# The byte distance between split weights and the activations they meet, changed from 32, 64, 96 and 128 to 48, 56, 72 and 80

## The reference

```python
def swiglu(h, w_gu, w_down):
    u = h @ w_gu                       # 1024 -> 2 x 2816
    g, v = u[..., :D_FF], u[..., D_FF:]
    return (jax.nn.silu(g) * v) @ w_down   # 2816 -> 1024

h = h + mixer(rmsnorm(h, g0))
h = h + swiglu(rmsnorm(h, g1), w_gu, w_down)   # six of these in all
```

## Time and profile before

| | us |
|---|---|
| median of 3 runs | 1706.4 |
| lowest, highest | 1705.34, 1708.17 |
| the profiled execution: its own time | 1707.63 |
| its span, first to last instruction | 1705.7 |
| outside the span | 1.9 |
| PE busy in the span | 1677.9 (98%) |
| DVE, ACT, POOL busy | 1265.5, 832.6, 375.4 |
| granted TensorE clock, mean | 0.999 of full |

### The profile page before, as it was taken

How to read it: one execution, slowest core, us unless ns; L and a number is a source line. 1 busy time by engine, 2 the same in 40 slices (tenths; PEclk the granted TensorE clock), 3 DMA queues, 4 the chain that set the end, 5 groups by cost and what they waited for, 6 DMA issues and landing times.

```text
span 1705.7 us, 31820 instructions
## 1 busy us (share of the span) xinstructions
PE 1677.9 (98%) x12958; PEld 1576.4 (92%) x12958; DVE 1265.5 (74%) x1657; ACT 832.6 (49%) x1104; POOL 375.4 (22%) x425
## 2 busy tenths in 40 slices
PE   7999999999999999999999999999999999999999
PEld 7789998898789999899989999998999999899998
DVE  7898889785868988788857866666666665676663
ACT  5865444343665444454444255444444445554442
POOL 0223012535505132610032130002100137330000
PEclk9999999999999999999999999999999999999999
DMA  8245567675206788555646445564455544335560
GB/s 321 107 141 211 210 219 262 232 281 190 77 2 205 244 267 300 183 191 194 228 166 235 137 162 177 193 220 176 152 193 204 215 150 168 125 126 198 202 230 33
DMA packets 50711, 321.02 MB, mean 188 GB/s; under 512 B 7696, under 2 KB 8912, under 8 KB 20144
## 3 DMA queue, kind: packets, MB, share of 16 engines
q1 hardware_dynamic: 36432, 280.61, 46.1%
q0 software_dynamic: 12736, 36.87, 6.7%
q10 hardware_dynamic: 1440, 2.10, 0.3%
HBM read 307.39 MB, written 10.09 MB: 186 GB/s over the span
## 4 chain that ended last, share of the span: by engine, by line
PE 87%; DVE 8%; ACT 2%; issue 2%; DMA 1%; POOL 0%; ACTq 0%; DVEq 0%; POOLq 0%
PE bank L2268 18%; PE bank L2262 17%; PE bank L2263 16%; PE bank L2264 16%; PE bank L2269 9%; DVE w_lo L1436 2%; PE bank L2549 1%; PE bank L2916 1%; PE bank L2868 1%; ACT w_hi L1006 1%; PE bank L2734 1%; PE bank L2623 1%; PE bank L2454 1%; PE bank L2559 1%; DVE rstd L1446 1%
## 5 line engine op out<-in xcount | busy, mean ns | idle before, releaser
L1436 DVE TENSOR_TENSOR w_lo<-raw,w_hi 128x1024 fp32r<-128x1024 f32 (+2 forms) x486 | 644.8, 1330 | 259.1 <-ACT w_hi L1006 257.9
L1006 ACT ACTIVATE w_hi<-raw 128x1024 fp32r<-128x1024 f32 (+2 forms) x486 | 538.2, 1117 | 546.7 <-PE bank L2264 323.0
L2262 PE MATMUL bank<-hg_hi,w_hi 128*128 128x256 f32 x2648 | 748.1, 283 | 12.3 <-DVE hg_lo L1441 10.4
L2263 PE MATMUL bank<-hg_lo,w_hi 128*128 128x256 f32 x2648 | 743.6, 281 | 0.0
L2264 PE MATMUL bank<-hg_hi,w_lo 128*128 128x256 f32 x2648 | 742.7, 280 | 0.0
L2262 PEld LDWEIGHTS bank<-hg_hi,w_hi 128*128 128x128 f32 x2648 | 500.6, 189 | 17.6 <-DVE w_lo L1436 11.5
L2264 PEld LDWEIGHTS bank<-hg_hi,w_lo 128*128 128x128 f32 x2648 | 501.1, 189 | 0.0
L2263 PEld LDWEIGHTS bank<-hg_lo,w_hi 128*128 128x128 f32 x2648 | 500.7, 189 | 0.2
L2268 PE MATMUL bank<-hid,w_hi 128*128 128x512 f32 x1056 | 370.2, 394 | 0.0
L2269 PE MATMUL bank<-hid,w_lo 128*128 128x256 f32 x1056 | 296.5, 281 | 0.0
L2268 PEld LDWEIGHTS bank<-hid,w_hi 128*128 128x128 f32 x1056 | 198.3, 188 | 46.4 <-issue 0.8
(11 more groups left out here) (412 smaller groups left out, 1900.3 us busy)
## 6 DMA issues: line engine op xcount, KB each, us to landing
raw<-in_w SPq DMA_DIRECT2D x189, 1024.0 KB, 4.8
raw<-in_w SPq DMA_DIRECT2D x48, 1408.0 KB, 6.5
raw<-in_w SPq DMA_DIRECT2D x8, 768.0 KB, 4.8
b_rows<-in_s_b_rows POOLq DMA_DIRECT2D x8, 512.0 KB, 8.0
l_rows<-s_powers POOLq DMA_DIRECT2D x64, 64.0 KB, 10.6
s_ca<-cp_s POOLq DMA_DIRECT2D x8, 512.0 KB, 4.6
s_ba<-ba_s POOLq DMA_DIRECT2D x8, 512.0 KB, 8.0
ba_slot<-s_ba POOLq DMA_DIRECT2D x8, 512.0 KB, 5.3
```

The costliest lines, as they stand in the source:

```text
L1006: act.activation(w_hi[s][:, 0:n], raw[r][:, c * n:(c + 1) * n], ACT.Copy).then_inc(hi_made, 1)
L1436: dve.tensor_tensor(w_lo[s][:, 0:n], raw[r][:, c * n:(c + 1) * n], w_hi[s][:, 0:n].bitcast(F32), ALU.subtract).then_inc(lo_made, 1)
L2262: pe.matmul(psum, w_hi_ap, x_hi_ap, start=first, stop=False, **kw)
L2263: pe.matmul(psum, w_hi_ap, x_lo_ap, start=False, stop=False, **kw)
```

## The change

The eight tiles of split weights become one tile, w_split, with eight views. Slot s starts at 2 * s * 1408 elements plus a skip of 4, 6, 10 or 12 elements, that is 16, 24, 40 or 48 bytes past a multiple of 512 from w_split's start, where w_split itself lies 32 bytes past hg's place modulo 512. w_hi and w_lo of a slot are 5632 bytes apart and have the same distance. The slots' distances become 48, 56, 72 and 80. The tiles between the weights and the region of the phases (vec, ones_d, sumsq, square, rms, rstd and the small ones) move down by 64 bytes, and `place[0] += 64` puts the region back where it was, so that hid, hq, mo_o, rec and all the others of the region keep their addresses. No instruction is added, taken away or moved in order.

```diff
@@ -189,10 +189,11 @@
         raw = [sb(f"raw{r}", [P, UNIT_MAX]) for r in range(RAW)]
         mask_s = sb("mask_s", [P, T + P], F32R, at=place[0] - (T + P) * 4)
         eps = sb("eps", [P, 1])
-        w_hi, w_lo = [], []
-        for s in range(SPLIT):
-            w_hi.append(sb(f"w_hi{s}", [P, UNIT_MAX // 2], F32R))
-            w_lo.append(sb(f"w_lo{s}", [P, UNIT_MAX // 2 + 8], F32R))
+        half_max = UNIT_MAX // 2
+        w_split = sb("w_split", [P, 2 * SPLIT * half_max + 16], F32R)
+        slot_at = [2 * s * half_max + skip for s, skip in enumerate((4, 6, 10, 12))]
+        w_hi = [w_split[:, at:at + half_max] for at in slot_at]
+        w_lo = [w_split[:, at + half_max:at + 2 * half_max] for at in slot_at]
         vec = sb("vec", [P, NVEC])
         ones_d = sb("ones_d", [P, P])
         sumsq = sb("sumsq", [P, T])
@@ -208,6 +209,7 @@
         joint = sb("joint", [P, 24])
         joint_gain, joint_scale, eps_2 = joint[:, 0:8], joint[:, 8:16], joint[:, 16:17]
 
+        place[0] += 64
         region = (place[0], nc.sbuf_usable_end // 32 * 32)
         ffn = Region(*region)
         hid = ffn.sb("hid", [P, 2, FT * T], F32R)
```

## The result

The changed kernel is slower by a hair. Its median is 1710.97 us (20 runs, 1709.72 to 1714.45), the kernel before's 1706.8 (20 runs), ratio 1.0024 with a 95% interval of 1.0016 to 1.0031. The span of the profiled execution goes from 1705.7 to 1710.6 us. The forecast was 1691 and 0.58 for faster. What came is a mild form of rival B.

What follows compares the result with a forecast made beforehand. PE was taken to bound the kernel, its rounds lasting as long as the matmuls' start-to-start pitch. 16 us less for 256-column matmuls and 1 more for pairs gave 15 less: 1692.6 profiled, 1691.4 median, range 1655 to 1722.

Steps and rivals of the forecast that it cites:

- rival B: Matmuls of 256 columns: 64's tight rhythm is lost, all four slots at mean 119.0 ns, 11 us more, 1717; chance 0.25.
- What bounds the kernel, and what the change can touch: Feed-forward rounds: PE is busy for all 117.00 us, so they follow the matmuls' pitch, the one thing the change can touch.
- the straight line between neighbours: Matmuls of 256 columns: pitches interpolated between sampled places, mean 115.8 ns against 117.7, over 8520 matmuls 16 us less.
- weakest step: Matmul pitch: assumed to vary smoothly in steps smaller than the 32 bytes sampled; nothing in the trace says so.
- D: Whole kernel: no effect that can be told, gains and losses cancel or all settle at about 117.8 ns, 1706; chance 0.12.
- Pairs: Pairs of matmuls, as in down projections: interpolated mean 350.1 ns against 349.3, over 1304 pairs 1 us more.
- Writing the slots, and the small tiles: ACT and DVE writing slots at new starting bytes, and vec, rstd and the rest moved 64 bytes: taken as no cost.
- Rival C: Weight loads: every load straddles memory lines and stalls, all at 120.1 and 351.8 ns, 23 us more, 1730; chance 0.05.
- the line rule behind it: Weight loads: 16-byte cachelines with a penalty for each crossing; by that 56 and 72 would suffer, 48 and 80 not.
- The independence of ports: PE's reads: the skill's independent ports for moving operand and weight load would give one pitch; trace rows disagreed, 2.73 against 2.88 us.

Runs made afterwards that it cites:

- the second and fourth experiments: Against the kernel before. Second: the same four distances given to other slots, 1705.4 us. Fourth: everything up to the weights 32 bytes higher, slot 3 at 64, 1698.85 us.

## Why the prediction was wrong

**What bounds the kernel, and what the change can touch.** Right. The rounds follow PE's pitch, and the pitch follows the distance between weights and activations: the earlier trace rows read so, and the second and fourth experiments confirm it against the slot and against the absolute address.

**The step that failed** is the straight line between neighbours for matmuls of 256 columns. It gave 116.2, 114.95, 115.3 and 116.9 ns at 48, 56, 72 and 80. Measured were 118.0, 117.8, 118.5 and 118.7: the mean is 118.3, not 115.8, and the term is about 4 us more (3.7 in the rounds alone) and not 16 less. The 113.7 at 64 is no valley whose slopes can be used. One element away, at 60 and 68, nothing of it is left in the kernel that tried them. The prediction named this as its weakest step and then let the sum rest on it. Two things in the trace spoke for caution: three of four sampled places stood at 118.3 to 120.1, so a place drawn at random was likely to be there; and the earlier trace rows showed 117.8 at 64 itself. A level of 117.8 for all four would have forecast 0.1 x 8520 = 1 us more. That is nearer than 16 less, though still below the 2.7 to 5.3 us that the interval of the ratio gives.

**Rivals B and D.** B had the right event, the tight rhythm lost within 8 bytes, and put 11 us on it by taking the mean of the three other places, 119.0. D had the same loss with all at 117.8 and 1 us. The places measured are at 118.3 on the mean, between the two. 4 us came, little more than the 3.4 that the prediction held a measurement could tell. That the weight load and the moving stream keep out of each other's way at 64, which B gives as the reason, no run shows.

**Pairs.** The mean was right, 350.1 forecast and 350.05 measured, and that was luck. The line between neighbours failed here too: it gave 349.5 at both 48 and 80, which took 347.0 and 352.9, and the two misses cancel. 60, with 366.8 ns, lies on no such line either. In time the down projections took 0.4 us more where 1 was put in for all pairs.

**Writing the slots, and the small tiles.** Both at nothing, both right: 1058 and 1258 ns as before, and no time back when the small tiles returned. The starts at 8 bytes past a multiple of 16 cost ACT and DVE nothing.

**Rival C** and the line rule behind it. The places 56 and 72 are the ones that straddle 16-byte lines, 48 and 80 are not. Their pitches are 117.8 and 118.5 against 118.0 and 118.7, so the start byte does not tell. Nor does it in the other kernels: 24 and 88, which both start 8 bytes past a multiple of 16, are at 121.6 and 114.5. The Trainium skill, "SBUF — State Buffer", "Specifications (TRN2)", has a penalty for each crossing of a 16-byte cacheline; no such penalty shows in the pitch here.

**The independence of ports.** The Trainium skill, "SBUF — State Buffer", "Who interferes with whom", lets PE's two reads run independently. By that the slots would have one pitch. Between 113.35 ns at 64 and 121.6 at 24 only places of weights differ, and a move of both operands together by 32 bytes changes the pitch by less than 0.1 ns, so for these float32r matmuls the measurement decides against it.

What stays open is what the two rhythms are inside PE. The runs show a period of 256 bytes and a dependence on how the stream came in, which fits two readers that get in each other's way and shift against each other when they do. No run looks inside a matmul, so this is argued and not shown. With all at 64 every change of rhythm came with a break in the stream, but what makes the stream loose behind one break and tight behind another is not settled, nor why the pitch at one distance depends on the distances of the neighbouring halves.

## What to carry to other kernels

Where a kernel is bound by back-to-back float32r matmuls, the distance in bytes between the stationary and the moving tile, modulo 256, is a tuning knob that was worth 1.4% here: moving nothing but tiles took this one from 1705.7 to 1681.6 us. The knob has no slope. A good place says nothing about the one 4 bytes away, so only sampled values may be used, each kind of matmul has its own best one, and a place must be tried in the mix in which it will run, since other neighbours moved the pitch of pairs at one distance by as much as 6.5 ns. The copies that refill weight slots give the length of each half for free, and a kernel whose slots lie at different distances is already a survey of them.

## What the runs showed of the hardware that was not expected

- The pitch of float32r matmuls of 256 columns goes from 113.35 to 121.6 ns with the places of the weights alone, at a mean granted clock of 0.997 to 1.0 in the profiled runs.
- It repeats within 0.05 ns after 256 bytes (118.48, 113.48, 120.13, 118.35 at 288 to 384, against 32 to 128), and changes by less than 0.1 ns when both operands move by 32 bytes (118.39, 113.35, 120.09 at 32, 64 and 96).
- At 64 and at 192 there are two stable values, 113.35 and 117.8, that last for many halves. The kernel before had the first in 65 of its 69 undisturbed halves at 64, and all at 192 had it in 1 of 276. With all at 64, in 88 unbroken stretches of up to 1007 matmuls, a rhythm never changed inside one.
- Pairs of 512 and 256 columns go from 346.7 ns (at 96, with 346.8 at 16 and 24) to 366.8 (at 60), with good places that differ from those of the other kind.
- The neighbouring halves count as well: pairs at 32 took 346.9 ns behind a half at 128 and 353.4 behind one at 64, and hg's matmuls at 96 took 120.1 behind 64 and 118.7 behind 128.
